# Moving the later modulation products of a two-layer diffusion layer stack into the recurrence stage

## The reference

```python
for l in range(DEPTH):                                   # DEPTH = 2
    mod = silu(c) @ w_mod[l] + b_mod[l]                  # 6 x 1024 values; the same with c_ctx
    sh1, sc1, g1, sh2, sc2, g2 = split(mod, 6)
    h = rmsnorm(x, ln1_w[l]) * (1 + sc1) + sh1
    a, b, c_ = heads(h @ w_in[l])                        # gated MLP | latent attention | recurrence
    x = x + g1 * (concat(mlp(a), attention(b), hgrn2(c_)) @ w_out[l])
    h = rmsnorm(x, ln2_w[l]) * (1 + sc2) + sh2
    x = x + g2 * peer(h, ...)                            # product-key route, gates, experts
```

## Time and profile before

| | us |
|---|---|
| runs, device time | 4206.97, 4220.92, 4219.45 |
| median | 4219.45 |
| profiled execution, its own time | 4212.56 |
| its span in the trace | 4210.7 |
| PE busy | 3895.2 (93%) |
| PEld busy | 3347.8 (80%) |
| DVE busy | 3417.3 (81%) |
| ACT busy | 2017.5 (48%) |
| POOL busy | 1151.7 (27%) |

### The profile page before, as it was taken

How to read it: one execution, slowest core, us unless ns; L and a number is a source line. 1 busy time by engine, 2 the same in 40 slices (tenths; PEclk the granted TensorE clock), 3 DMA queues, 4 the chain that set the end, 5 groups by cost and what they waited for, 6 DMA issues and landing times. The chain is left out here.

```text
span 4210.7 us, 68057 instructions
## 1 busy us (share of the span) xinstructions
PE 3895.2 (93%) x24022; PEld 3347.8 (80%) x24022; DVE 3417.3 (81%) x6336; ACT 2017.5 (48%) x3796; POOL 1151.7 (27%) x1095
## 2 busy tenths in 40 slices
PE   7969989988899999999999888898988999999998
PEld 6854468977788888888888777336876999999998
DVE  5387948877699999999999965665976999999998
ACT  4467532278344444444444355654276444444443
POOL 0000000078244334433343300000075333333332
PEclk9979999899999999999999998999988999999999
DMA  5101211256899999999999811112246999999997
GB/s 195 56 16 65 90 65 46 68 164 176 301 376 375 376 373 383 373 384 369 374 373 373 335 62 50 40 50 75 81 121 222 376 369 375 370 374 370 376 370 290
DMA packets 247019, 1018.48 MB, mean 242 GB/s; under 512 B 17121, under 2 KB 115521, under 8 KB 146641
## 3 DMA queue, kind: packets, MB, share of 16 engines
q0 software_dynamic: 85296, 599.59, 36.9%
q1 hardware_dynamic: 161504, 416.31, 27.3%
HBM read 963.34 MB, written 52.43 MB: 241 GB/s over the span
## 5 line engine op out<-in xcount | busy, mean ns | idle before, releaser
L558 PE MATMUL psA<-h_hi,split 128*128 128x448 f32 (+3 forms) x5536 | 1495.6, 348 | 101.9 <-DVE xT L2738 54.5
L558 PEld LDWEIGHTS psA<-h_hi,split 128*128 128x128 f32 x5536 | 1001.3, 191 | 213.1 <-issue 127.6
L1467 POOL DMA_INDIRECT rows<-rows,pick_i x512 | 795.7, 1554 | 1163.2 <-DVE y_tok L2759 645.7
L2097 DVE TENSOR_TENSOR split<-raw,split 128x1024 fp32r<-128x1024 f32 x596 | 727.3, 1220 | 314.6 <-ACT split L1511 304.2
L558 PE MATMUL psA<-h_lo,split 128*128 128x448 f32 (+3 forms) x2768 | 952.6, 344 | 0.0
L1511 ACT ACTIVATE split<-raw 128x1024 fp32r<-128x1024 f32 x596 | 628.2, 1054 | 329.3 <-DMA raw<-expert_pairs 147.3
L558 PE MATMUL psV<-W_hi,split 128*128 128x320 f32 (+3 forms) x2560 | 667.7, 326 | 3.5 <-DVE W_lo L2733 3.4
L2747 DVE CUSTOM_DVE_ANT_1 rows<-rows,h_wide 128x1024 f32<-128x1024 f32 x512 | 624.2, 1219 | 13.9 <-DMA rows<-rows,pick_i 11.5
L2759 DVE SCALAR_TENSOR_TENSOR y_tok<-rows,pick_w,y_tok 128x1024 f32<-128x1024 f32 x444 | 568.8, 1281 | 5.9
L558 PEld LDWEIGHTS psA<-h_lo,split 128*128 128x128 f32 x2768 | 528.8, 191 | 34.1
L558 PE MATMUL psA<-W_hi,split 128*128 128x448 f32 (+1 forms) x1792 | 513.7, 342 | 0.0
(11 more groups left out here) (338 smaller groups left out, 5200.0 us busy)
## 6 DMA issues: line engine op xcount, KB each, us to landing
raw<-expert_pairs SPq DMA_DIRECT2D x256, 1024.0 KB, 7.2
gates<-g_buf SPq DMA_DIRECT2D x22, 2048.0 KB, 9.0
raw<-tiles SPq DMA_DIRECT2D x84, 512.0 KB, 3.3
raw<-mod_tiles SPq DMA_DIRECT2D x80, 512.0 KB, 3.2
g_in<-gates POOLq DMA_DIRECT2D x32, 896.0 KB, 9.2
g_in<-gates POOLq DMA_DIRECT2D x32, 640.0 KB, 5.8
mod_w<-mod_pairs SPq DMA_DIRECT2D x8, 1024.0 KB, 19.9
rows<-rows,pick_i POOLq DMA_INDIRECT x512, 8.6
```

Of the source, the lines that this page charges most:

```text
L558: ins = nc.tensor.matmul(out_, lhsT, rhs, start=start, stop=stop)
L1467: nc.gpsimd.indirect_dma_start(rows[l][:, b, :], None, (rows0, rows1)[l], bass.IndirectOffsetOnAxis(pick_i[:, u:u + 1], 0))\
L2097: V.tensor_tensor(split_lo[:, n % SPLIT].rearrange("p k n -> p (k n)"), raw[:, n % RAW, :], split_hi[:, n % SPLIT].rearrange("p k n -> p ( ...
```

## The change

All 80 later tiles are multiplied in the recurrence stage, in the form of the opening, as 40 pairs of 1 MB: `LATER_PAIRS` is 24 in layer 0 and 16 in layer 1, two pairs per unit. Nothing of the modulation is left in attention or route.

- PE: `later_rows_of(u)` (16 matmuls of 256 columns, which the trace counts twice since float32 takes two passes) stands ahead of the scores of unit u+1, and `turn_later(u)` (four matmuls with two columns) behind the output of unit u; for the last unit the turn stands ahead of the output.
- ACT: one broadcast copy of the conditions per layer at the stage's start (`later_wide`), and one 128 x 512 copy per unit (`copy_later`), behind the next unit's decays.
- DVE: in place of the products in attention, one addition of the bias ahead of the stage's last collect.
- PSUM: the later tiles take one bank of the second bank pair and the turned values the other, so that all output groups use the first pair, and a group's first output waits until DVE has collected the group before.
- SP: two pair loads are in flight, and each pair is refilled when PE has passed it (`mod_passed`). The `cond_late` load, its Silu, and the loads of tiles in attention and route are gone; the first two expert pairs are loaded without waiting for modulation.

```diff
-MOD_OWN, MOD_NEXT = (32, 16), (24, 8)
-MOD_CALLS = ((0, 1, 2, 3), (0, 2))
-MOD_STEP = ((0,) * 8 + tuple(range(3, 3 + 6 * 16, 6)), (0,) * 8)
+LATER_PAIRS = (24, 16)
...
-        def mod_tile(dst, slot):
-            pe.wait_ge(raw_landed[slot], seen.upto(raw_landed[slot], 16))
-            for c in range(KD):
-                ins = nc.tensor.matmul(dst, raw[:, slot, c * P:(c + 1) * P], c_raw[:, c], start=c == 0, stop=c == KD - 1)
-            ins.then_inc(mod_passed, 1)
...
+            def later_rows_of(u):
+                for i in range(2):
+                    slot = (OUT0[l] + 2 * i) % RAW
+                    pe.wait_ge(raw_landed[slot], seen.upto(raw_landed[slot], 16))
+                    for c in (0, 2, 4, 6, 1, 3, 5, 7):
+                        g = slice(32 * (c // 2), 32 * (c // 2) + 32)
+                        ins = nc.tensor.matmul(psA[g, (fo + 2) % 4, 2 * P * i:2 * P * (i + 1)], later_wide[:, c].rearrange("p r j -> p (r j)"),
+                                               raw[:, slot:slot + 2, c * P:(c + 1) * P], start=c % 2 == 0, stop=c % 2 == 1)
+                    ins.then_inc(mod_passed, 1)
+
+            def turn_later(u):
+                pe.wait_ge(mod_rows_copied, KD + units_before(l) + u + 1)
+                for i in range(4):
+                    ins = nc.tensor.matmul(psA[:, (fo + 3) % 4, 8 * u + 2 * i:8 * u + 2 * i + 2], later_rows[:, i], turn_sum,
+                                           start=True, stop=True)
...
             for u, (_, s, tt, _) in enumerate(units):
+                later_rows_of(u)
                 if u + 1 < len(units):
                     scores(u + 1)
                 if u == 0:
                     pe.wait_ge(state_ready, seen.upto(state_ready))
                     pe.wait_ge(qexp_ready, seen.upto(qexp_ready))
+                else:
+                    if tt == s // P:
+                        pe.wait_ge(psum_A_free, seen.upto(psum_A_free, 4))
+                    if u == len(units) - 1:
+                        turn_later(u)
                 if tt == s // P:
-                    fo = seen.bank(psum_A_free)
                     out_bank[l].append(fo)
-                    pe.wait_ge(psum_A_free, seen.upto(psum_A_free, 2))
                 output(u, fo)
+                if u < len(units) - 1:
+                    turn_later(u)
...
+            def copy_later(u):
+                act.wait_ge(mod_passed, 2 * (units_before(l) + u + 1))
+                A(later_rows[:].rearrange("p i n -> p (i n)"), psA[:, later_bank, :], ACT.Copy).then_inc(mod_rows_copied, 1)
...
-                V.tensor_tensor(o_, o_, psA[:, f + 1, 0:n], ALU.add).then_inc(psum_A_free, 2)
+                V.tensor_tensor(o_, o_, psA[:, f + 1, 0:n], ALU.add).then_inc(psum_A_free, 4)
...
-                V.tensor_tensor_reduce(prod_late[:], w, cond_late[:, 0], 1.0, 0.0, ALU.mult, ALU.add, mod_sum[:, i, 0:1])
-                V.tensor_tensor_reduce(w, w, cond_late[:, 1], 1.0, 0.0, ALU.mult, ALU.add, mod_sum[:, i, 1:2]).then_inc(mod_passed, 1)
```

More of the change, by code:

```diff
@@ L1335, in load_pairs @@
                 load_pair(EX0[l] + 2 * p, l * EXPERT_TILES // 2 + p)
[L1337 to L1346, removed]
-                    sp.wait_ge(mod_passed, seen.upto(mod_passed))
[L1349 to L1356, removed]
@@ new lines, in later_modulation @@
+        def later_modulation(l):
+            first, n0, rounds = sum(LATER_PAIRS[:l]), OUT0[l], LATER_PAIRS[l] // 2 - 1
+            for m in range(2):
+                b = (n0 + 2 * m) % RAW
+                sp.wait_ge(hi_done, n0 + 2 * m + 2 - RAW)
+                sp.wait_ge(lo_done, n0 + 2 * m + 2 - RAW)
+                sp.dma_start(raw[:, b:b + 2, :], later_pairs[first + m]).then_inc(raw_landed[b], 16)
+            with sp.Fori(0, rounds) as i:
+                seen.enter(i, {mod_passed: 2})
+                for m in range(2):
+                    b = (n0 + 2 * m) % RAW
+                    sp.wait_ge(mod_passed, seen.upto(mod_passed))
+                    sp.dma_start(raw[:, b:b + 2, :], later_pairs[i * 2 + (first + 2 + m)]).then_inc(raw_landed[b], 16)
+            seen.leave(rounds)
+            for n in range(RAW):
+                if n % 2 == 0:
+                    sp.wait_ge(mod_passed, seen.upto(mod_passed))
+                b = (n0 + n) % RAW
+                sp.dma_start(raw[:, b, :], tiles[tile_row(n0 + n)]).then_inc(raw_landed[b], 16)
@@ L1358, in route_loads @@
         def route_loads(l):
-            first, count, n0 = NEXT0[l] - MOD_FIRST, MOD_NEXT[l], EX0[l]
             by_block = gates.rearrange("q p t n -> t p q n")
             blocks = [t // TB for t in dense_tokens(l)[::GROUPS]]
-            for n in range(RAW):
-                sp.wait_ge(hi_done, n0 - RAW + n + 1)
-                sp.wait_ge(lo_done, n0 - RAW + n + 1)
-                sp.dma_start(raw[:, (n0 + n) % RAW, :], mod_tiles[first + n]).then_inc(raw_landed[(n0 + n) % RAW], 16)
-            loaded = [0]
@@ L1369, in loads_to @@
-            def loads_to(step):
-                while loaded[0] < count and MOD_STEP[l][loaded[0]] <= step:
-                    n = loaded[0]
-                    loaded[0] += 1
-                    b = (n0 + n) % RAW
-                    sp.wait_ge(mod_passed, seen.upto(mod_passed))
-                    if n + RAW < count:
-                        sp.dma_start(raw[:, b, :], mod_tiles[first + RAW + n]).then_inc(raw_landed[b], 16)
-                    elif n % 2:
-                        sp.dma_start(raw[:, b - 1:b + 1, :], expert_pairs[l * EXPERT_TILES // 2 + (n + RAW - count) // 2])\
-                            .then_inc(raw_landed[b - 1], 16)
+            for p in range(2):
+                load_pair(EX0[l] + 2 * p, l * EXPERT_TILES // 2 + p)
@@ L1871, in attention @@
             act.sem_inc(v_ready, 1)
-            act.wait_ge(cond_landed, 16 * (l + 1))
-            A(cond_late[:], cond_late[:], ACT.Silu).then_inc(cond_rows_ready, 1)
-            act.wait_ge(cond_rows_ready, l + 1)
             for h in range(-1, BH):
@@ L1897, in attention @@
             act.wait_ge(head_ready, seen.upto(head_ready))
-            for b in range(RAW):
-                seen.n[raw_landed[b]] += 16 * MOD_OWN[l] // RAW
+            for m in range(LATER_PAIRS[l]):
+                seen.n[raw_landed[(OUT0[l] + 2 * m) % RAW]] += 16
             mix_high(MIX_ORDER[0:4])
@@ L1993, in route @@
                 seen.upto(psum_A_free, 2)
-            for b in range(RAW):
-                seen.n[raw_landed[b]] += 16 * MOD_NEXT[l] // RAW
             act.wait_ge(g_stored[0], seen.n[g_stored[0]])
```

97 lines of the change are left out of this document (33 added, 64 removed).

## The result

The changed kernel takes 4244.68 us (median of five, 4239.79 to 4251.21), the kernel before 4219.45 in the same runs: a ratio of 1.0065, 95% interval 1.005 to 1.008. The forecast was 4200.5, so it missed by 44 us and in the sign. The profiled execution took 4249.47 us with a span of 4247.6.

What follows compares the result with a forecast made beforehand. DVE was taken to bound the recurrence, PE attention and the route's start; gains 7.5 + 3.8 + 8.7 + 14 = 34 us against 15 paid gave 19 less than 4219.45: 4200.5 us, range 4181 to 4224.

Steps and rivals of the forecast that it cites:

- The loads: Recurrence: pair loads land just in time and cost nothing; at most 9 us if each takes the median 7.3.
- rival E: Recurrence: the loads set the unit, +9, and last pairs come late, +2; 4211 us in all, chance 0.09.
- my price of the end: End of each layer's recurrence: turns, last two pairs and ACT's copy delay the last output by 4.4 us.
- The clock: PE in the recurrence: a fuller PE leaves the slow clock; few slow units, 1.0 us per layer.
- Rival D: Recurrence: PE's work becomes the bound, slow units cost 3.2 us each; twelve give +17, about 4237; chance 0.15.
- The rest of the recurrence: Recurrence cost from end, bank pair, conditions' copy and clock: 8.4 us in layer 0, 6.6 in layer 1.
- the shared bank pair: Recurrence: outputs wait for the previous group's collect; 2.6 us in layer 0 (0.8 each mid-stage), 0.8 in layer 1.
- Attention: Attention without DVE's products: 7.5 us gained in layer 0, 3.8 in layer 1.
- waits for the maxima: Attention: of PE's 6.4 us waiting for row maxima in layer 0, 4.3 go; in layer 1 half of 6.8.
- The route: Route without modulation tiles: 8.7 us gained at the two layers' starts, 14 in layer 0's gate steps.
- The 16 tiles among the gate steps: Layer 0's gate steps: removing PE's 16 modulation tiles gains 14 us, between nothing and 20.5.
- rival B: Gate steps: ACT paces them, so the 16 tiles were hidden and 14 becomes 2; 4212 us, chance 0.14.

Runs made afterwards that it cites:

- e1_first_loads: Changed kernel, but only each layer's first two pairs are loaded and later units reread them (wrong values); all matmuls, copies and turns stay: 4186.21 us, ratio 0.9932.
- the hybrid: Against the changed kernel: only the route's tiles moved into the recurrence, mostly one pair per unit behind the next scores, attention's products left on DVE: 4190.17 us, ratio 0.9937.
- e8_hybrid_early: Against the hybrid: layer 0's first two pairs made ahead of the state products, none in its last two units: 4192.58 us, ratio 0.9945.
- e3_spread: Changed kernel with only each unit's second pair moved behind the next unit's scores, the first staying ahead: 4216.82 us, ratio 1.0002.
- e2_half_strips: Changed kernel with each pair multiplied by only four of eight contraction blocks (incomplete values), loads, copies and turns kept: 4226.87 us, ratio 1.0034.
- e4_tail: Changed kernel with each layer's last turn behind the last output and the bias addition behind the last collect: 4232.08 us, ratio 1.0048.
- e5_front: Changed kernel's 40 pairs rearranged: one batch before state products, none in last units, second pairs behind next scores, turns behind outputs: 4207.17 us, ratio 0.9977.
- e7_both_behind: Changed kernel with both pairs' strips behind the next unit's scores in place of ahead of them: 4234.53 us, ratio 1.0048.

## Why the prediction was wrong, point by point

**The loads: the step that failed.** The prediction said: "the second lands behind the first, near 7.1, and PE wants it 0.9 later than the first: just in time. I cost it at nothing", with an upper price of 9 us over both layers, and the rival E at 0.09 with 11 us. They cost 51.6 us (`e1_first_loads`). The landing time was not far off (6.8 in the median, 8.3 at most, against 7.1). The two errors were in what I did with it. I compared it with a unit of 6.15 us as if a slot were refilled the moment the unit begins, while the second slot's round trip is landing (up to 8.3) plus strips (1.07 to 1.94) plus whatever stands in PE's queue; two units take 16 to 18 us in place of 12.3. And I used 6.15 for all units, though the last distances of a layer are 3.9 and 2.8 us, shorter than the 4.8 us of a pair alone: 22.0 of layer 0's 35.9 us are there, 16.7 of which go with the loads. For these last units my price of the end (4.4) had strips, copy and turn, but took the last pairs as loaded. The slow strips behind the waits and the pauses without a releaser are part of the 51.6, and the prediction had neither. Rival E named the right mechanism and its sign (PE waits for `raw`), but at a fifth of its cost.

For the 4.4 us of a pair alone the prediction drew on the Trainium skill ("DMA: Bandwidth & Descriptors", "Anatomy of one DMA"), which gives its fit of 2.0 us plus the bytes at 436 GB/s for DMAs that GpSimd issues. SP issues the pairs here, and one alone took 4.8 us. The prediction's own inference, that two in flight would keep up, is what failed: issued less than 1 us behind another, a load took 7.8 us in the median.

**The clock: right in direction, but it hung on the loads.** I expected a fuller PE to leave the slow level and put 1.0 us per layer; with the loads out of the way the clock was 0.91, up from 0.74. With them it was 0.77. That the Trainium skill ("TensorE: Matmul & The Clock Gate", Part 1) has activity release the throttle agrees with 0.74 and 0.91, where PE worked 57.72 of 90.10 and 79.05 of 90.00 us. It does not order all the rows: the changed kernel's PE worked 94.07 of 120.00 us at 0.77, the hybrid's 63.13 of 86.99 at 0.92. What sets the clock here stays open. Rival D had PE's work as the cause and the slow clock as its price. Its 4237 came nearest to the measured 4244.68, but only as a number: its symptom was there (DVE waited for scores in mid-recurrence), its cause was not, since all of PE's added work stood in `e1_first_loads` too.

**The rest of the recurrence: right, somewhat high.** 8.4 and 6.6 us forecast, 5.3 and 5.0 measured without loads. At the end of layer 0 the strips (1.93), the hand-over with the copy (0.72) and the turn (1.05) are as priced, and all of the 5.3 is there (16.1 against 10.8). In the middle the shared bank pair (2 x 0.8) cost 0.1 and slow units nothing.

**Attention: the number right in layer 0 (7.5, measured 7.0), wrong in layer 1 (3.8, measured -0.1 in the changed kernel and 1.6 without loads).** In layer 0 PE's idle time ahead of out-projection fell from 5.66 to 3.04 us, as priced (2.7). But its waits for the maxima fell only from 6.4 to 4.3 us, not by 4.3 and not to near zero, so part of the agreement is luck; most of the rest is PE's own busy time in the stage (222.62 to 221.17 us). Over the kernels without the products the stage takes 237.8 to 243.0 us, against 247.0 before, so 7.0 is one value of several. In layer 1 the waits fell from 9.0 to 6.8 us over the whole stage, so most of them never stood behind products; halving them was a guess.

**The route: right, somewhat low.** The starts gave 6.7 + 4.1 = 10.8 (forecast 8.7). The 16 tiles among the gate steps gave 16.4 (forecast 14), and 16.4 to 17.1 in every other kernel of the study but `e8_hybrid_early` (13.6). Holding the layers' times per step side by side gave 16.8; rival B, which set ACT's mean work against the six steps and came to 2, is refuted.

## What to carry to other kernels

A load that is issued when its slot is passed has a round trip: landing, the work that reads it, and what stands ahead of that work in its engine's queue. Set that against the shortest unit in which the slot is wanted, not the mean one, and let two slots be passed at different times, so that one load is not issued right behind the other: the same bytes then cost 0.9 us in the middle of layer 0's stage in place of 13.8. Before work is moved into idle time, ask what it cost where it was: DVE's 48 tiles in attention cost 7 us on the path, and moving them took 24 of the 40 loads, while the 32 tiles on PE in the route cost 27, and their 16 loads fit for 5.

## What the runs showed of the hardware

Two 1 MB loads in flight that SP issued are not served alike. Of 26 issued less than 1 us behind another, the first landed after 4.7 to 5.6 us, hardly later than one alone (4.8), and the second after 6.5 to 8.6; from a distance of 4 us on the second took 4.8 to 5.1 in the median. All the same, with the loads 2.2 to 5.0 us apart (`e3_spread`) 295 GB/s were moved over 50 us.

PE's granted clock went with the loads within one and the same program of matmuls: 0.91 without them, 0.77 with them, where PE waited 15 us in 120 for pairs. The time spent waiting does not tell the clock by itself: the hybrid's PE waited 18.6 us in 87 for DVE, no wait longer than 3.0, and had 0.92.

PE can also stand still for 2.1 to 4.3 us with nothing in the trace to wait for, in the recurrences of the changed kernel, `e2_half_strips`, `e3_spread` and `e4_tail`. In the kernel before, the hybrids and `e1_first_loads` the longest such pause is 1.3 us. A 16 KB piece of the instruction queue starts to move within 2 us of the start of each long pause. That the pair loads hold it up is argued, not shown; `e5_front` and `e7_both_behind` load as much and have no pause above 1.5 us.
